# Seeding, casts and first-quad order in a two-block transformer kernel with seven-product quads

## The reference

```python
h2 = rmsnorm(x, norm2_g[l])
x = x + jnp.square(jax.nn.relu(h2 @ w_mlp_in[l])) @ w_mlp_out[l]     # 2048 -> 8192 -> 2048
...
h2 = rmsnorm_2(x, g_mlp[l])
x = x + jnp.square(jax.nn.relu(h2 @ w_up[l])) @ w_down[l]            # the same in block two
```

## Time and profile before

| | |
|---|---|
| median of 3 runs | 2803.37 us (2803.25 to 2803.71) |
| the profiled execution: its own time | 2803.97 us |
| its span, first to last instruction | 2802.2 us |
| PE busy | 2783.2 us, 99% of the span |
| PEld busy | 2294.5 us, 82% |
| DVE busy | 2229.2 us, 80% |
| ACT busy | 1578.9 us, 56% |
| mean granted TensorE clock | 0.999 |

### The profile page before, as it was taken

One profiled execution on the slowest core, in us unless ns is written; L12 is line 12 of the kernel. 1 busy time (PEld: TensorE's weight loads), 2 busy tenths in 40 slices (PEclk: granted clock), 3 DMA queues, 4 the chain that ended last, 5 costly groups with the idle time before them and its releaser, 6 DMA issues.

```text
span 2802.2 us, 34047 instructions
## 1 busy us (share of the span) xinstructions
PE 2783.2 (99%) x13066; PEld 2294.5 (82%) x13066; DVE 2229.2 (80%) x2506; ACT 1578.9 (56%) x1796; POOL 2.6 (0%) x7
## 2 busy tenths in 40 slices
PE   9999999999999999999999999999999999999998
PEld 7888878888887888888888888888888888888887
DVE  6698855656778999999967678877678999999985
ACT  6644445544455666666656444444455666666664
POOL 0000000000000000000000000000000000000000
PEclk9999999999999999999999999999999999999999
DMA  9576646656876677766677666667676766676774
GB/s 329 157 226 203 204 151 213 199 192 202 265 214 223 210 248 246 238 218 235 219 251 218 225 199 217 200 206 223 206 235 202 250 219 233 218 248 233 248 234 148
DMA packets 372643, 617.01 MB, mean 220 GB/s; under 512 B 23041, under 2 KB 96385, under 8 KB 371841
## 3 DMA queue, kind: packets, MB, share of 16 engines
q1 hardware_dynamic: 372048, 614.51, 67.6%
q10 hardware_dynamic: 432, 0.32, 0.0%
HBM read 577.26 MB, written 2.10 MB: 207 GB/s over the span
## 4 chain that ended last, share of the span: by engine, by line
PE 89%; DVE 7%; issue 1%; ACT 1%; DMA 1%; ACTq 0%; DVEq 0%
PE ACC L927 76%; PE TB L934 7%; PE ACC L934 5%; DVE WLS L1704 1%; DVE FG L1719 1%; DVE TSL L1730 1%; DVE FG L1721 1%; DVE FG L1723 1%; DVE YBL L1730 1%; DVE YAL L1730 1%; DMA RAW<-in_w_up_dram 1%; ACT X L1549 0%; DMA RAW<-in_w_mlp_in_dram 0%; PE TB L1054 0%; DVE XTL L2272 0%
## 5 line engine op out<-in xcount | busy, mean ns | idle before, releaser
L1704 DVE TENSOR_TENSOR WLS<-RAW,WHS 128x1024 fp32r<-128x1024 f32 (+1 forms) x1023 | 1174.8, 1166 | 406.2 <-ACT WHS L1205 404.8
L1205 ACT ACTIVATE WHS<-RAW 128x1024 fp32r<-128x1024 f32 (+1 forms) x1023 | 1009.3, 1012 | 702.5 <-PE ACC L927 573.9
L927 PE MATMUL ACC<-WHS,XTH 128*128 128x512 f32 (+1 forms) x1692 | 658.3, 389 | 0.0
L927 PE MATMUL ACC<-WLS,XTH 128*128 128x512 f32 (+1 forms) x1692 | 655.4, 387 | 0.0
L927 PE MATMUL ACC<-WHS,XTL 128*128 128x512 f32 (+1 forms) x1692 | 655.3, 387 | 0.0
L927 PEld LDWEIGHTS ACC<-WHS,XTH 128*128 128x128 f32 x1692 | 317.9, 188 | 65.5 <-issue 0.4
L927 PEld LDWEIGHTS ACC<-WHS,XTL 128*128 128x128 f32 x1692 | 317.8, 188 | 64.8
L927 PEld LDWEIGHTS ACC<-WLS,XTH 128*128 128x128 f32 x1692 | 317.9, 188 | 64.0
L927 PE MATMUL ACC<-WHS,YAH 128*128 128x512 f32 x864 | 336.4, 389 | 0.0
L927 PE MATMUL ACC<-WLS,YAH 128*128 128x512 f32 x864 | 336.3, 389 | 0.0
L927 PE MATMUL ACC<-WHS,YAL 128*128 128x512 f32 x864 | 336.3, 389 | 0.0
(11 more groups left out here) (397 smaller groups left out, 3347.3 us busy)
## 6 DMA issues: line engine op xcount, KB each, us to landing
RAW<-in_w_in_dram SPq DMA_DIRECT2D x255, 512.0 KB, 4.5
RAW<-in_w_mlp_out_dram SPq DMA_DIRECT2D x128, 512.0 KB, 5.8
RAW<-in_w_down_dram SPq DMA_DIRECT2D x128, 512.0 KB, 5.6
RAW<-in_w_mlp_in_dram SPq DMA_DIRECT2D x115, 512.0 KB, 4.5
RAW<-in_w_up_dram SPq DMA_DIRECT2D x115, 512.0 KB, 4.6
RAW<-in_w_gate_dram SPq DMA_DIRECT2D x96, 512.0 KB, 4.3
YT<-HT SPq DMA_DIRECT2D x208, 128.0 KB, 3.2
RAW<-in_w_branch_dram SPq DMA_DIRECT2D x48, 512.0 KB, 4.1
```

The costliest lines, as they stand in the source:

```text
L927: ins = e.matmul(ACC[:, 2 * (b % 2) + half, 0:n], p[:, k, xs], q[:, t, 0:n], start=(k == 0 and m == 0 and b not in SEEDED), stop=(k == nk ...
L1205: e.activation(halves(WHS, u)[:, :, 0:n], RAW[u % NRAW][:, ts, 0:n], ACT.Copy).then_inc(hi, 1)
L1704: e.tensor_tensor(l, r, h, ALU.subtract).then_inc(lo, 1)
```

## The change

It has four parts, in both MLPs.

1. Blocks o(j,0), o(j,1) and o(j,2) are seeded and come back by ScalarE; o(j,3) isn't and comes back by VectorE's addition. For j below 6 that step stands one unit later than ScalarE's did. The seed of o(j,0) stands at the last unit of h(j+1,0).
2. The two high casts of the sums made ahead are two steps, behind two units, instead of one.
3. The sevens of the first pair of an MLP are quads 0, 2, 4 and 6.
4. In quad 0 of each pair the products of the second unit come in the order T4, S_2, S_4, then the wait for the other accumulator, S_1, S_3; and in the first pair the waits for the sums of x are three, each ahead of the product that needs it.

```diff
-    FIRST_I = (0, 2, 3, 5)
+    FIRST_I = (0, 2, 4, 6)
...
-            for c in (1, 2, 3):
-                if (tag, j, c) != ("2", 7, 3):
-                    SEEDED[B["o" + tag, j, c]] = len(SEEDED) + 1
+            for c in (0, 1, 2):
+                SEEDED[B["o" + tag, j, c]] = len(SEEDED) + 1
...
-                at(("ev", "o" + tag), last("o" + tag, j, c) + (j < 7))
+                at(("ev", "o" + tag), last("o" + tag, j, c) + (j < 7) + (j < 6 and c == 3))
                 b = B["o" + tag, j, c]
                 if b in SEEDED:
-                    at(("seed", tag), UE[b - 2] + (2 if c > 1 else 1 - (c == 0)))
+                    at(("seed", tag), UE[b - 2] + (2 if c > 1 else 1 - (c == 0 and j < 7)))
...
-            at("ahead_hi", h - 28)
+            at("ahead_hi", h - 28, 2)
...
-            at("ahead_hi", h - 15)
+            at("ahead_hi", h - 14, 2)
...
-            at("ahead_hi", h - 5)
+            at("ahead_hi", h - 5, 2)
...
             if m == 0:
                 if rec.first:
-                    e.wait_ge(xs_lo, 3 * (n // 7 + 1))
+                    e.wait_ge(xs_lo, 3 * (n // 7) + 1)
                     e.wait_ge(acc[b0 % 2], b0 // 2)
...
+            if rec.first:
+                e.wait_ge(t_lo, 2 * rec.q + 2)
+                three(TB[2][:, :], x(2 * i + 1, 1), weight_sums(T4), True, False)
+                e.wait_ge(xs_lo, 3 * (n // 7) + 2)
+                three(acc_bank(b0, 1), sums(S_2), weight_sums(T2), True, False)
+                e.wait_ge(xs_lo, 3 * (n // 7) + 3)
+                three(TB[1][:, :], sums(S_4), w[1], True, False)
+                e.wait_ge(acc[(b0 + 1) % 2], (b0 + 1) // 2)
+                three(acc_bank(b0 + 1, 0), sums(S_1), weight_sums(T1), True, False)
+                three(acc_bank(b0 + 1, 1), sums(S_3), weight_sums(T3), True, False).then_inc(mm, 1)
+                return
             three(TB[1][:, :], sums(S_4), w[1], i == 0, False)
             e.wait_ge(t_lo, 2 * rec.q + 1)
             three(acc_bank(b0, 1), sums(S_2), weight_sums(T2), rec.first, rec.last)
-            if rec.first:
-                e.wait_ge(acc[(b0 + 1) % 2], (b0 + 1) // 2)
```

More of the change, by code:

```diff
@@ L1211, in sums_high @@
             e.activation(parts[0][:, T_PARTS[0], :], tr[:, T_PARTS[0], :], ACT.Copy).then_inc(t_hi, 1)
+            yield
             e.wait_ge(t_sum, 3 * rec.q + 3)
             e.activation(parts[0][:, T_PARTS[1], :], tr[:, T_PARTS[1], :], ACT.Copy).then_inc(t_hi, 1)
+            yield
         def ahead_hi():
             for rec in AHEAD_OF.values():
-                sums_high(rec)
-                yield
+                yield from sums_high(rec)
         def stream(u, front):
@@ L1234, in stream @@
                 if odd(v) and not SEVEN[v][0].ahead:
-                    sums_high(SEVEN[v][0])
+                    for _ in sums_high(SEVEN[v][0]):
+                        pass
             front()
```

## The result

The changed kernel takes 2878.97 us (median of 4 runs, 2877.71 to 2879.09), the kernel before 2803.54 us beside it (2803.25 to 2805.41). The ratio is 1.0267, with a 95% interval of 1.0249 to 1.0284: slower by 2.7%. The profiled execution took 2878.99 us.

A forecast was written before the change was run, and what follows sets the result against it. TensorE, 99% busy, was taken as the bound, so only its gaps and matmuls count. 2803.97 + 54.1 - 3.4 = 2854.7, with 9 for the clock 2863.7, less 0.6 for the runs' median: 2863 us, range 2851 to 2879 us.

The forecast's parts named there:

- What bounds the kernel: Whole kernel: TensorE is busy 99% of 2802.2 us, so only its gaps and its matmuls can move the time.
- The eviction: Quad 0 of 12 pairs: TensorE waits for VectorE's late addition of o(j,3), a stall of 5.34 us each.
- The term of 54.1 us: 12 pairs after an o block: each loses 5.45 us instead of 0.94, 4.51 more.
- Quad 6: Quad 6 of a pair: VectorE's low parts are there at 982.5, TensorE comes at 983.66, so the old wait goes.
- The edits priced at nothing: Seeding o(j,0), its eviction on ScalarE and splitting the casts made ahead: claimed to cost nothing.
- The first pairs: First pair of each MLP: shorter start wait and no later wait, 1.7 us won each, 3.4 us together, between 0 and 3.9.
- The clock: The 12 gaps at quad 0: TensorE's clock may fall to half while idle, 9 us, bounds 0 to 26 us.
- A fall in every second gap: The 12 gaps at quad 0: the assumed share of gaps in which the clock falls, part of the 9 us.
- 1.5 us for each: The 12 gaps at quad 0: the assumed loss at half pace per clock fall, part of the 9 us.
- The sign that the prediction named for being low: Behind the gaps: the prediction is low if rows of 0.43 us spacing last longer than 4 us.
- falls in every gap and stays low for long: Rival on the 12 gaps: the clock falls each time, 2854 + 26 = 2880 us, chance 0.12.
- The rival with the clock holding: Rival on the 12 gaps: the clock doesn't fall, 2854 us, chance 0.14.

The follow-up runs named there:

- the filled kernel: The changed kernel with 22 matmuls into an unused bank ahead of the wait for the second accumulator, in each of 12 pairs: 2853.66 us, ratio 1.0174.
- the kernel with 14 matmuls: The changed kernel with 14 matmuls into an unused bank ahead of the wait for the second accumulator, in each of 12 pairs: 2864.96 us, ratio 1.0219.

## Why the prediction was right, and where it was off

**What bounds the kernel.** Right. TensorE's gaps and its rows at half pace are the difference; VectorE's busy time moved by 0.5 us and ScalarE's by 2.0.

**The eviction.** Right in place, number and size. Forecast were 12 waits for line 2227 of 5.2 us and a stall of 5.34 us; measured were 12, 5.20 us and 5.36 us. The walk along VectorE gave 957.10 - 950.98 = 6.12 us from YAL to the addition, and it took 6.13. The forecast holds because every instruction ahead of the addition stood in the trace with its duration. Moving it ahead of them made the wait vanish, which shows that cause. The term of 54.1 us measured 12 x (5.36 + 0.11 - 0.94) = 54.4.

**Quad 6.** Right: the low parts were to be there 1.2 us ahead of TensorE, and were 1.7. With the eviction early or undone the wait comes back, 0.68 us in pair 2, so it was the stall that gave VectorE this time.

**The edits priced at nothing.** With the seeding as changed and the eviction early, the ratio is the same 0.9982 as with the seeding undone; the seeding costs nothing that can be told within the interval of 0.1%, some 2.7 us. The split casts (part 2) have not been run alone; both kernels have them, and neither is slower than before.

**The first pairs.** Right. Forecast were 3.4 us won, 1.7 in each MLP; the timelines show 1.79 and 2.06, 3.85 us. The rest came in the second MLP, where before one more row came late, by 0.3 us at 2181.98, with a slow row behind it; the forecast doesn't count them. What the sum leaves for the first pairs is 2803.97 + 54.4 + 24.4 - 2878.99 = 3.8 us. That it agrees so closely is in part luck: two differences of 0.9 us outside the terms of the sum cancel. The changed kernel came 0.94 us later to its first pair (863.81 against 862.87), and the kernel before took 84.17 us instead of 83.24 for one pair of the second MLP. The kernel with these parts and not part 1 has the ratio 0.9982, which is 5.0 us of the 2804.56 measured beside it, 2.2 to 7.6 by the interval.

**The clock.** The mechanism was right, the size wrong: this is the term of the sum that was mis-sized, 9 us forecast, 24.4 measured by rows and 25.3 by the filled kernel. Two choices failed. "A fall in every second gap" was a fall in each of 12. "1.5 us for each" was 24.4 / 12 = 2.0. I had one fall in the trace, 4.3 us behind the last matmul, and held it against 5.2 us as if it were a limit that a gap just passes. The changed kernel has falls between 2.3 and 5.0 us behind the last matmul (windows of a quarter of a us). The sign that the prediction named for being low came too: half pace lasted 3.1 to 6.1 us behind the gaps, about 4.0 or longer in 8 of 12. So the rival "falls in every gap and stays low for long" with its 2880 us and its chance of 0.12 was the case that came true, and not the forecast of 2863 us with 0.67. The range reached 2879 only because it took most of that rival in, and the measured 2878.97 lies 0.03 us inside it: that is luck. The rival with the clock holding (2854 us) is what the filled kernel runs at: 2853.66.

The Trainium skill, page "TensorE: Matmul & The Clock Gate", section "Why this matters for your kernels", cited in the prediction, warns of idle gaps of a few microseconds. By that rule the clock should have been counted in each gap. This case agrees, with a fall in 12 of 12 gaps of 5.20 and of 3.16 us; and in gaps of 2.02 us it still fell in 7 of 12.

## What to carry to other kernels

Before a step is moved to another engine, walk that engine's rows from the last point where it can't be early and add up the durations to the new place: here six instructions, 6.13 us, foreseen to 0.01 us, and the cure was the same step six instructions higher. Price a stall of TensorE not only by its length: here every gap with 3.16 us of idle time or more cost some 2 us more for the clock, and 7 of 12 with 2.02 us cost 1.6. Take a single fall in a trace as one sample, not as a limit. Where the stall can't be removed, matmuls into an unused bank that leave about 1 us of idle time gave the clock's share back, here 25 of 75 us.

## What was not expected of the hardware

- The clock fell in 12 of 12 gaps of 5.2 us, and of 3.16 us, in 7 of 12 of 2.02 us, in none of 1.12 us. Equal gaps of one kernel had their falls between 2.3 and 5.0 us behind the last matmul, and lost between 1.4 and 2.8 us to it.
- It can fall after the gap: in the kernel with 14 matmuls about 0.3 us after TensorE had gone on (1045.01), and so in 6 of its 7 falls. Cutting the idle time of 12 gaps from 5.20 to 3.16 us left all 12 falls, and the time was only 1.65 us lower.
- Two VectorE subtractions of 1.82 us together took 2.91 us while GpSimd subtracted 128x512 in 2.20 us, 60 times of 60.
